# A fused three-layer kernel on one core: a new order of the first three weight strips, x in smaller pieces, ten idle matmuls, and the first norm's sum on another engine

## The chip, the cores and the metric

The kernel runs on one core of one Trainium2 chip. A core has a tensor engine (PE, matrix products, results in the PSUM banks), a vector engine (DVE), a scalar engine (ACT), GpSimd (POOL) and a sync engine (SP) that mostly issues DMAs. Each engine runs its own instructions in order, and they meet by semaphores. The metric is the device time of one execution in microseconds; lower is better. The kernel before took 1658.15 us, the median of three runs (1657.92 to 1658.49).

## The reference

Three transformer layers on x of 512 tokens by 1024 features, all in float32. What the change touches is the first step of layer 0:

```python
mem_n = rmsnorm(mem, mem_norm)
mem_kv = mem_n @ w_mem_kv[i]                      # keys and values of the memory attention
h = rmsnorm(x, norm_mix[i])
proj = h @ a_w_in[i]
u, b_gate, c_gate, q_mem = jnp.split(proj, [768, 1536, 2304], axis=-1)
y_tok = _short_conv(u, b_gate, c_gate, a_conv_w[i])   # b_gate * conv3(c_gate * u)
y_mem = _mem_attention(q_mem, mk, mv)
x = x + jnp.concatenate([y_tok, y_mem], axis=-1) @ w_out
```

A gated FFN, a layer with sliding-window attention, a second FFN, and a layer with sparse attention and retention follow. The change leaves them alone.

## The kernel before

**Arithmetic.** Activations lie feature-major: x is eight tiles (k = 0..7) of 128 features by 512 tokens. A product in float32 is made of three faster ones. An operand is split into a rounded high half and the rest: for the weight `w_hi` (a copy on ACT) and `w_lo = raw - w_hi` (DVE), for the activation `a_hi` (ACT, x times the norm's gain) and `a_lo` (DVE). A **strip** n is 128 output features: one weight block of 512 KB, and for each k three matmuls, hi·hi, hi·lo and lo·hi, 24 in all, into one PSUM bank. The rms factor of a token is multiplied in afterwards, when DVE reads the bank (`l0_epilogue`), so PE may start before the norm is known.

**The norm.** ACT squares the tiles of x into two buffers `sq`, POOL adds them up in `acc` (`squares`), PE sums `acc` over the features (`sums`, four matmuls of one column), DVE scales (`variance`), POOL raises to the power -1/2 (`power`), DVE makes a diagonal (`diagonal`, `diag`), PE spreads it over the partitions (`spread`), and ACT copies it to `rstd`.

**Strips.** Strips 0 and 1 are the memory queries, 2 to 4 the first conv triple (u, c, b), 5 to 12 keys and values of the memory (256 columns each), 13 to 27 the other conv triples. Strip n uses slot n % 2 of `w_hi` and `w_lo` and slot n % 4 of `raw`. ACT's `split(n)` waits until strip n - 2 has left PE (`blk_done`), DVE's follows ACT's, and SP's `load(n)` waits until DVE has split strip n - 3.

**The order.** Each engine has its list written out in the source. At the outset SP and ACT issue the transfers of x (four pieces of 512 KB, two tiles each) and of the first weights; PE runs strip 0, then strip 1, and so on; the sums of the first norm stand before strip 3 and its spread before strip 4. On ACT, `conv_out(0)` (the high half `y_hi` of the first conv tile) stands at n = 5 of its loop, and the squares of the memory in pairs at n = 4 to 7.

Of the kernel before, what the change touches and what calls it, by code (L numbers as in the profile page):

```python
# [102 lines left out]
def build(nc, a, out):  # L103
# [393 lines left out]
    with nc.Block() as block:  # L497
# [88 lines left out]
        def _(pool):  # L586
# [95 lines left out]
        def _(act):  # L682
            act.dma_start(gains[:], a["gains"]).then_inc(gains_in, 16)
            for j in (0, 2):
                act.dma_start(x[:, 2 * j:2 * j + 2, :], a["xT"][:, 2 * j:2 * j + 2, :])\
                    .then_inc(x_in[j], 16)
# [98 lines left out]
            for n in range(N_QM0, N_OUT0 + 1):  # L785
# [1691 lines left out]
```

## Time and profile before

| what | value |
|---|---|
| median of three runs | 1658.15 us |
| the profiled execution: its own time | 1657.95 us |
| its span in the trace | 1656.0 us |
| PE busy | 1621.1 us (98%) |
| DVE, ACT, POOL busy | 872.4, 572.6, 139.4 us |
| granted clock of PE, mean | 0.997 |
| DMA, mean over the span | 92 GB/s |

The span is what the trace covers; the execution's own time is 1.95 us longer. PE is matrix products, PEld the loading of weights beside them; a name with q, as SPq, is the engine's sequencer issuing DMAs. A row of the timeline begins with start and duration in us; in brackets stands how long the engine was idle before, and what ended that. A matmul's duration contains its drain, so successive ones overlap; their pitch is read from the starts.

### The profile page before, as it was taken

What the parts mean: (1) busy time and instruction counts of PE and PEld (TensorE: products, weight loads), DVE (VectorE), ACT (ScalarE), POOL (GpSimd) and SP (SyncE); (2) the same over time, 40 slices, a digit from 0 to 9 for tenths busy, and PEclk for the clock granted to TensorE, in tenths of its full rate; (3) what the DMA queues carried; (4) which work ended last, traced back from release to release, by engine and by line L of the source; (5) the groups of instructions that cost most, each with busy time, mean ns of one, the idle gap of its engine ahead of it and who ended that gap; (6) DMA issues with size and microseconds to landing.
All of it is one profiled execution on the core that took longest, in us unless ns stands there. A gap on an engine that the chain in (4) does not pass through costs nothing.

```text
span 1656.0 us, 20546 instructions
## 1 busy us (share of the span) xinstructions
PE 1621.1 (98%) x7706; PEld 1299.1 (78%) x7706; DVE 872.4 (53%) x1174; ACT 572.6 (35%) x965; POOL 139.4 (8%) x123
## 2 busy tenths in 40 slices
PE   7999999999999999999999999999999999999997
PEld 6877888888888876678888888887677677888885
DVE  5566654444523466764444443337666655555443
ACT  5333432232222345543323323322355541233222
POOL 3100200000000000030000001113211101000001
PEclk9999999999999999999999999999999999999999
DMA  5322323222333331132322332252111111233231
GB/s 213 128 76 89 97 90 101 99 91 101 113 105 99 69 111 33 38 110 89 101 100 90 101 123 95 88 203 66 64 54 50 51 64 32 83 103 100 90 102 77
DMA packets 43246, 152.70 MB, mean 92 GB/s; under 512 B 5325, under 2 KB 8622, under 8 KB 42670
## 3 DMA queue, kind: packets, MB, share of 16 engines
q1 hardware_dynamic: 42114, 148.36, 27.1%
q10 hardware_dynamic: 1068, 3.47, 0.7%
q8 instruction: 42, 0.69, 0.2%
q14 instruction: 22, 0.18, 0.0%
HBM read 149.42 MB, written 2.39 MB: 92 GB/s over the span
## 4 chain that ended last, share of the span: by engine, by line
PE 58%; DVE 3%; issue 1%; ACT 0%; POOL 0%; DVEq 0%; ACTq 0%; POOLq 0%
PE ps L1767 16%; PE ps L1769 15%; PE ps L1768 15%; PE ps L2114 1%; PE ps L2128 1%; PE ps L2150 1%; PE ps L2174 1%; PE ps L2214 1%; PE ps L2213 1%; PE ps L2215 1%; PE ps L1942 1%; PE ps L2062 0%; PE ps L1974 0%; PE ps L2164 0%; PE ps L1959 0%
## 5 line engine op out<-in xcount | busy, mean ns | idle before, releaser
L1767 PE MATMUL ps<-a_hi,w_hi 128*128 128x512 f32 (+1 forms) x1368 | 544.7, 398 | 10.9 <-DVE a_lo L1077 8.6
L1769 PE MATMUL ps<-a_hi,w_lo 128*128 128x512 f32 (+1 forms) x1368 | 534.6, 391 | 0.0
L1768 PE MATMUL ps<-a_lo,w_hi 128*128 128x512 f32 (+1 forms) x1368 | 534.5, 391 | 0.0
L1072 DVE TENSOR_TENSOR w_lo<-raw,w_hi 128x1024 fp32r<-128x1024 f32 (+4 forms) x262 | 334.6, 1277 | 257.7 <-ACT w_hi L695 252.2
L695 ACT ACTIVATE w_hi<-raw 128x1024 fp32r<-128x1024 f32 (+4 forms) x262 | 274.7, 1048 | 313.7 <-PE ps L1769 289.0
L1767 PEld LDWEIGHTS ps<-a_hi,w_hi 128*128 128x128 f32 (+1 forms) x1368 | 257.0, 188 | 73.3 <-issue 17.0
L1769 PEld LDWEIGHTS ps<-a_hi,w_lo 128*128 128x128 f32 (+1 forms) x1368 | 256.9, 188 | 55.3
L1768 PEld LDWEIGHTS ps<-a_lo,w_hi 128*128 128x128 f32 (+1 forms) x1368 | 257.2, 188 | 52.4 <-issue 1.0
L1098 DVE TENSOR_TENSOR tmp<-ps,rstd 128x512 f32<-128x512 f32 x121 | 83.4, 691 | 182.6 <-PE ps L1769 172.4
L1767 PE MATMUL ps<-g_hi,w_hi 128*128 128x512 f32 x352 | 137.0, 389 | 0.0
L1768 PE MATMUL ps<-g_lo,w_hi 128*128 128x512 f32 x352 | 137.0, 389 | 0.0
L1769 PE MATMUL ps<-g_hi,w_lo 128*128 128x512 f32 x352 | 137.0, 389 | 0.0
L602 POOL TENSOR_TENSOR acc<-acc,sq 128x512 f32<-128x512 f32 (+1 forms) x40 | 52.2, 1306 | 537.8 <-ACT sq L704 535.9
L845 ACT ACTIVATE g_hi<-tmp 128x512 f32 (+1 forms) x44 | 27.8, 632 | 198.6 <-DVE tmp L1272 198.6
L1767 PEld LDWEIGHTS ps<-g_hi,w_hi 128*128 128x128 f32 x352 | 66.1, 188 | 13.8
L1769 PEld LDWEIGHTS ps<-g_hi,w_lo 128*128 128x128 f32 x352 | 66.1, 188 | 13.8
L1768 PEld LDWEIGHTS ps<-g_lo,w_hi 128*128 128x128 f32 x352 | 66.1, 188 | 13.6
L1111 DVE TENSOR_TENSOR x<-x,ps 128x512 f32<-128x512 f32 (+1 forms) x40 | 27.4, 686 | 87.8 <-PE ps L1769 87.8
L841 ACT ACTIVATE tmp<-tmp 128x512 f32<-128x512 f32 x44 | 27.8, 632 | 122.8 <-DVE tmp L1098 122.8
L1077 DVE SCALAR_TENSOR_TENSOR a_lo<-x,gains,a_hi 128x512 fp32r<-128x512 f32 (+1 forms) x40 | 38.5, 973 | 33.8 <-ACT a_hi L707 33.8
L1276 DVE TENSOR_TENSOR g_lo<-tmp,g_hi 128x512 f32 (+1 forms) x44 | 30.5, 692 | 38.8 <-ACT g_hi L845 38.8
L707 ACT ACTIVATE a_hi<-x,gains 128x512 fp32r<-128x512 f32 (+1 forms) x40 | 28.1, 714 | 59.0 <-DVE x L1111 55.6
(271 smaller groups left out, 1739.8 us busy)
## 6 DMA issues: line engine op xcount, KB each, us to landing
raw<-w SPq DMA_DIRECT2D x135, 512.0 KB, 3.4
raw<-w8b SPq DMA_DIRECT2D x70, 512.0 KB, 3.4
raw<-w_down SPq DMA_DIRECT2D x32, 704.0 KB, 4.0
w<-cmp_w SPq DMA_DIRECT2D x2, 2048.0 KB, 10.9
raw<-w_out_first SPq DMA_DIRECT2D x8, 320.0 KB, 2.9
raw<-w_nsa_o SPq DMA_DIRECT2D x8, 256.0 KB, 2.6
out<-o_t SPq DMA_DIRECT2D x4, 512.0 KB, 3.2
bias<-rel_scratch SPq DMA_DIRECT2D x8, 192.0 KB, 7.1
```

The lines of the kernel that those rows point to most:

```text
L602: pool.tensor_tensor(acc[:, 0:cols], acc[:, 0:cols], sq[:, k % 2, 0:cols], ALU.add).then_inc(acc_ready, 1)
L695: act.activation(w_hi[:, slot, 0:w], raw[:, raw_slot, 0:w], ACT.Copy)\
L707: act.activation(a_hi[:, k, :], x[:, k, :], ACT.Copy, scale=gains[:, g, bass.ds(k, 1)])\
L841: act.activation(tmp[:, 2 * j, :], tmp[:, 2 * j, :], ACT.Silu).then_inc(silu_ready, 1)
L845: act.activation(g_hi[:, m, :], tmp[:, 2 * j + 1, :], ACT.Copy).then_inc(g_hi_ready, 1)
L1072: dve.tensor_tensor(w_lo[:, slot, 0:w], raw[:, raw_slot, 0:w], w_hi[:, slot, 0:w].bitcast(F32), ALU.subtract).then_inc(w_lo_ready, 1)
L1077: dve.scalar_tensor_tensor(a_lo[:, k, :], x[:, k, :], gains[:, g, bass.ds(k, 1)], a_hi[:, k, :].bitcast(F32), ALU.mult, ALU.subtract)\
L1098: ins = dve.tensor_tensor(dst, ps[:, bank, :], rstd[:], ALU.mult)
L1276: dve.tensor_tensor(g_lo[:, m, :], tmp[:, 2 * j + 1, :], g_hi[:, m, :].bitcast(F32), ALU.subtract)\
L1767: pe.matmul(o, wh, a_h, start=start and at == 0, stop=False)
L1768: pe.matmul(o, wh, a_l, start=False, stop=False)
L1769: ins = pe.matmul(o, wl, a_h, start=False, stop=stop and at == kt - 1)
```

## The change

- **x** comes in eight pieces of 256 KB, tile 0 on ACT's queue, the other seven on SP's. SP's queue begins with the gains and the first halves of weights 0 and 1; the second halves stand behind tile 3.
- **Strips 0 and 1** run side by side (`first_strips`): for each k three matmuls of strip 0, then three of strip 1. ACT and DVE split both weights in halves between the tiles of x.
- **Strip 2** has `third_hi` and `third_lo` in place of slot 0, so its split needn't wait for strip 0.
- **PE** begins with ten products of 128 columns of the all-ones tile, whose result nobody reads.
- **The first norm**: DVE adds the squares (`first_square`), not POOL. `sums` stands behind k = 6 of strip 2, `spread` behind k = 3 of strip 3.
- **Later pieces**: `conv_out(0)` and its low half move to n = 8 and 9; the squares of the memory move to n = 3 and 4, four at a time; the epilogues of strips 0 to 2 move from n = 4 to n = 3.

```diff
+WARM = 10
@@ SP
-            sp.dma_start(raw[:, 0, 0:mid], a["w8"][0][:, 0:mid]).then_inc(first_in, 16)
-            for j in (1, 3):
-                sp.dma_start(x[:, 2 * j:2 * j + 2, :], a["xT"][:, 2 * j:2 * j + 2, :]).then_inc(x_in[j], 16)
...
+            sp.dma_start(gains[:], a["gains"]).then_inc(gains_in, 16)
+            for n in range(2):
+                sp.dma_start(raw[:, n, 0:mid], a["w8"][n][:, 0:mid]).then_inc(first_in[n], 16)
+            for k in range(1, KT):
+                sp.dma_start(x[:, k, :], a["xT"][:, k, :]).then_inc(x_in[k], 16)
+                if k == 3:
+                    for n in range(2):
+                        sp.dma_start(raw[:, n, mid:KT * P], a["w8"][n][:, mid:KT * P]).then_inc(raw_in[n], 16)
@@ POOL
-            squares(V_MIX0)
+            clear(V_MIX0)
@@ ACT
-            act.dma_start(gains[:], a["gains"]).then_inc(gains_in, 16)
-            for j in (0, 2):
-                act.dma_start(x[:, 2 * j:2 * j + 2, :], a["xT"][:, 2 * j:2 * j + 2, :])\
-                    .then_inc(x_in[j], 16)
+            act.dma_start(x[:, 0, :], a["xT"][:, 0, :]).then_inc(x_in[0], 16)
...
+            act.wait_ge(raw_in[2], 16)
+            act.activation(third_hi[:], raw[:, 2, 0:KT * P], ACT.Copy).then_inc(w_hi_ready, 1)
             for k in range(KT):
                 square(V_MIX0, k, k % 2, x[:, k, :], first=k < 2)
-                if k == 3:
-                    split(2, KT * P)
+                if k == 5:
+                    split(3, KT * P)
@@ DVE
+            def first_square(k):
+                dve.wait_ge(sq_ready, k + 1)
+                dve.wait_ge(acc_ready, 1 + k)
+                dve.tensor_tensor(acc[:], acc[:], sq[:, k % 2, :], ALU.add).then_inc(acc_ready, 1)
@@ PE
+            def first_strips():
+
+                for k in range(KT):
+                    pe.wait_ge(a_lo_ready, k + 1)
+                    for n in range(2):
+                        if k == 0:
+                            pe.wait_ge(first_lo, n + 1)
+                        if k == KT // 2:
+                            pe.wait_ge(w_lo_ready, n + 1)
...
+                        pe.matmul(o, wh, a_hi[:, k, :], start=k == 0, stop=False)
+                        pe.matmul(o, wh, a_lo[:, k, :], start=False, stop=False)
+                        ins = pe.matmul(o, wl, a_hi[:, k, :], start=False, stop=k == KT - 1)
+            def begin_beside(n, at):
+
+                if n == 2 and at == 6:
+                    sums(V_MIX0)
+                if n == 3 and at == 3:
+                    spread(V_MIX0)
...
-            pe.wait_ge(half_ready, 1)
-            for n in range(N_QM0, N_OUT0):
+            for i in range(WARM):
+                pe.matmul(ps[:, stat_bank, 0:P], ones[:], ones[:], start=True, stop=True)
+            first_strips()
+            for n in range(N_CONV0, N_OUT0):
```

On DVE at the outset, before the change (`x4` is four in a row, the bracket names the semaphores waited for):

```order
L1144 TENSOR_TENSOR w_lo<-raw,w_hi 128x512 [waits first_hi]
L1077 SCALAR_TENSOR_TENSOR a_lo<-x,gains,a_hi 128x512 [waits a_hi_ready] x2
L1150 TENSOR_TENSOR w_lo<-raw,w_hi 128x512 [waits w_hi_ready]
L1077 SCALAR_TENSOR_TENSOR a_lo<-x,gains,a_hi 128x512 [waits a_hi_ready] x4
L1072 TENSOR_TENSOR w_lo<-raw,w_hi 128x1024 [waits w_hi_ready]
L1077 SCALAR_TENSOR_TENSOR a_lo<-x,gains,a_hi 128x512 [waits a_hi_ready] x2
L1072 TENSOR_TENSOR w_lo<-raw,w_hi 128x1024 [waits w_hi_ready]
L1226 SCALAR_TENSOR_TENSOR mem_lo<-memx,gains,mem_hi 128x256 [waits mem_hi_ready] x4
```

And after it:

```order
L1091 SCALAR_TENSOR_TENSOR a_lo<-x,gains,a_hi 128x512 [waits a_hi_ready]
L1160 TENSOR_TENSOR w_lo<-raw,w_hi 128x512 [waits first_hi] x2
L1091 SCALAR_TENSOR_TENSOR a_lo<-x,gains,a_hi 128x512 [waits a_hi_ready] x3
L1165 TENSOR_TENSOR w_lo<-raw,w_hi 128x512 [waits w_hi_ready] x2
L1091 SCALAR_TENSOR_TENSOR a_lo<-x,gains,a_hi 128x512 [waits a_hi_ready] x4
L1188 TENSOR_TENSOR third_lo<-raw,third_hi 128x1024 [waits w_hi_ready]
L1171 TENSOR_TENSOR acc<-acc,sq 128x512 [waits acc_ready,sq_ready] x8
L1086 TENSOR_TENSOR w_lo<-raw,w_hi 128x1024 [waits w_hi_ready]
L1175 SCALAR_TENSOR_TENSOR mem_lo<-memx,gains,mem_hi 128x256 [waits mem_hi_ready] x4
L1097 TENSOR_SCALAR var<-ps 128x4 [waits norm_sum]
L1175 SCALAR_TENSOR_TENSOR mem_lo<-memx,gains,mem_hi 128x256 [waits mem_hi_ready]
L1103 TENSOR_TENSOR diag<-ident,rs 128x512 [waits norm_pow,const_in]
```

The split of strip 1 moved forward among the tiles, and the eight sums now stand between the splits of strips 2 and 3.

On ACT from strip 5's split on, before the change (`y_hi` is `conv_out(0)`, `sq<-memx` a square of the memory):

```order
L695 ACTIVATE w_hi<-raw 128x1024 [waits blk_done,raw_in1]
L802 ACTIVATE table<-ps 12x383 [waits table_mm]
L804 ACTIVATE sinks<-sinks 128x12 [waits small_in]
L712 ACTIVATE rstd<-ps 128x512 [waits norm_spread]
L704 ACTIVATE sq<-memx 128x256 [waits acc_ready] x2
L695 ACTIVATE w_hi<-raw 128x1024 [waits blk_done,raw_in2]
L783 ACTIVATE y_hi<-y_s 128x512 [waits conv_step]
L704 ACTIVATE sq<-memx 128x256 [waits acc_ready] x2
L695 ACTIVATE w_hi<-raw 128x1024 [waits blk_done,raw_in3]
```

And after it:

```order
L698 ACTIVATE w_hi<-raw 128x1024 [waits blk_done,raw_in1]
L816 ACTIVATE table<-ps 12x383 [waits table_mm]
L818 ACTIVATE sinks<-sinks 128x12 [waits small_in]
L707 ACTIVATE sq<-memx 128x256 [waits acc_ready] x4
L698 ACTIVATE w_hi<-raw 128x1024 [waits blk_done,raw_in2]
L698 ACTIVATE w_hi<-raw 128x1024 [waits blk_done,raw_in3]
L698 ACTIVATE w_hi<-raw 128x1024 [waits blk_done,raw_in0]
L698 ACTIVATE w_hi<-raw 128x1024 [waits blk_done,raw_in1]
L795 ACTIVATE y_hi<-y_s 128x512 [waits conv_step]
```

`y_hi` moved from behind the split of strip 6 to behind that of strip 9, and no square stands between the splits of strips 6 to 9 any more.

## Rows read from the trace of the kernel before

**Rows 1.** The page, part 1: busy us (share of the span) xinstructions.

```profile
PE 1621.1 (98%) x7706; PEld 1299.1 (78%) x7706; DVE 872.4 (53%) x1174; ACT 572.6 (35%) x965; POOL 139.4 (8%) x123
```

**Rows 2.** Waits of PE: line, releaser, us in total, times, longest.

```profile
PE ps L1767 <- DVE a_lo L1077: 8.6, 1, 8.6
PE ps L1767 <- DVE w_lo L1072: 3.9, 5, 2.1
```

**Rows 3.** Timeline of PE at the outset.

```profile
8.63 0.77 PE L1767 MATMUL ps<-a_hi,w_hi 128*128 128x512 f32 x1 [8.63 <-DVE a_lo L1077]
...
14.71 0.39 PE L1769 MATMUL ps<-a_hi,w_lo 128*128 128x512 f32 x1
```

**Rows 4.** Timeline of PE, starts of strips 2, 3, 5, 7; sums and spread.

```profile
22.46 0.39 PE L1767 MATMUL ps<-a_hi,w_hi 128*128 128x512 f32 x1
...
27.90 0.95 PE L1779 MATMUL ps<-ones,acc 128*128 128x1 f32 x8
...
29.48 0.51 PE L1767 MATMUL ps<-a_hi,w_hi 128*128 128x512 f32 x1 [0.63 <-DVE w_lo L1072]
...
42.38 0.28 PE L1767 MATMUL ps<-mem_hi,w_hi 128*128 128x256 f32 x1
...
50.37 0.36 PE L1767 MATMUL ps<-mem_hi,w_hi 128*128 128x256 f32 x1 [2.08 <-DVE w_lo L1072]
...
54.38 0.58 PE L1779 MATMUL ps<-ones,acc 128*128 128x1 f32 x4 [0.91 <-POOL acc L602]
...
57.78 0.59 PE L1786 MATMUL ps<-diag,ones 128*128 128x256 f32 x2
```

**Rows 5.** DMA issues about 1.1 us: size, us from issue to landing.

```profile
x<-xT SPq DMA_DIRECT2D x1, 512.0 KB, 5.4
raw<-w SPq DMA_DIRECT2D x1, 256.0 KB, 2.8
gains<-gains ACTq DMA_DIRECT2D x1, 32.0 KB, 3.0
```

**Rows 6.** Windows, 10 to 12 us: busy us by engine, clock, DMA share, GB/s.

```profile
10.00:12.00 2.00, 2.00 (x6) 1.57 (x5) 2.00 (x4) 2.00 (x4) 0.00 (x0) 1.00 1.03 422
```

**Rows 7.** The page, part 6: count, size, median us to landing.

```profile
raw<-w_nsa_o SPq DMA_DIRECT2D x8, 256.0 KB, 2.6
```

**Rows 8.** Timeline of ACT, at the outset and at the first conv_out.

```profile
3.58 0.63 ACT L757 ACTIVATE w_hi<-raw 128x512 fp32r<-128x512 f32 x1
...
6.97 1.33 ACT L707 ACTIVATE a_hi<-x,gains 128x512 fp32r<-128x512 f32 x2 [2.77 <-DMA x<-xT]
...
46.31 0.63 ACT L783 ACTIVATE y_hi<-y_s 128x512 fp32r<-128x512 f32 x1 [2.62 <-DVE y_s L1190]
```

**Rows 9.** Timeline of DVE: a_lo, two splits, mem_lo, the two diags.

```profile
9.88 2.74 DVE L1077 SCALAR_TENSOR_TENSOR a_lo<-x,gains,a_hi 128x512 fp32r<-128x512 f32 x4
...
19.44 2.31 DVE L1072 TENSOR_TENSOR w_lo<-raw,w_hi 128x1024 fp32r<-128x1024 f32 x1 [4.23 <-ACT w_hi L695]
...
28.21 1.22 DVE L1072 TENSOR_TENSOR w_lo<-raw,w_hi 128x1024 fp32r<-128x1024 f32 x1
29.34 1.66 DVE L1226 SCALAR_TENSOR_TENSOR mem_lo<-memx,gains,mem_hi 128x256 fp32r<-128x256 f32 x4
...
33.43 0.69 DVE L1089 TENSOR_TENSOR diag<-ident,rs 128x512 f32<-128x512 f32 x1 [1.22 <-POOL rs L609]
...
56.78 0.43 DVE L1089 TENSOR_TENSOR diag<-ident,rs 128x256 f32<-128x256 f32 x1 [0.83 <-POOL rs L609]
```

**Rows 10.** Timeline of POOL: the first norm's eight sums, the power.

```profile
14.52 12.69 POOL L602 TENSOR_TENSOR acc<-acc,sq 128x512 f32<-128x512 f32 x8 [13.03 <-ACT sq L704]
32.29 1.03 POOL L609 TENSOR_TENSOR rs<-var,half 128x4 f32<-128x4 f32 x1 [5.08 <-DVE var L1083]
```

**Rows 11.** Groups of PE by form: busy us, mean ns of one.

```profile
L2164 PE MATMUL ps<-qr,kr 128*128 128x512 f32 x8 | 4.1, 592 | 0.0
...
L2164 PE MATMUL ps<-qr,kr 128*128 128x128 f32 x8 | 1.5, 274 | 0.0
```

More of the change, by code:

```diff
@@ L253, in build @@
     raw_in = [sem(f"raw_in{i}") for i in range(RAW)]
-    x_in = [sem(f"x_in{i}") for i in range(4)]
+    x_in = [sem(f"x_in{i}") for i in range(KT)]
     mem_in = sem("mem_in")
@@ L257, in build @@
     const_in = sem("const_in")
-    first_in = sem("first_in")
+    first_in = [sem(f"first_in{i}") for i in range(2)]
     first_hi = sem("first_hi")
@@ L792, in _ @@
                     mem_evac(0, MEM_AT[0][n - MEM_LAG[0]], 1)
-                if kind == "b":
+                if kind == "b" and i:
                     conv_out(i)
+                if n == 8:
+                    conv_out(0)
                 if n in (1, 2):
@@ L1146, in _ @@
             for k in range(KT):
                 operand(k, G_MIX0, k + 1)
[L1148 to L1154 removed]
+                if k == 0:
+                    first_half(0)
+                    first_half(1)
@@ new lines, in _, with conv_low @@
+                if k == 3:
+                    second_half(0)
+                    second_half(1)
+            dve.wait_ge(w_hi_ready, 3)
+            dve.tensor_tensor(third_lo[:], raw[:, 2, 0:KT * P], third_hi[:].bitcast(F32), ALU.subtract)                .then_inc(w_lo_ready, 1)
+            for k in range(KT):
+                first_square(k)
+            split(3, KT * P)
+            def conv_low(i):
+                dve.wait_ge(yc_hi_ready, i + 1)
+                dve.tensor_tensor(y_lo[:, i, :], y_s[:], y_hi[:, i, :].bitcast(F32), ALU.subtract)\
+                    .then_inc(yc_lo_ready, 1)
@@ L1759, in strip @@
                         pe.wait_ge(late[0], late[1])
-                    if isinstance(n, int) and n == 0 and k == kt // 2:
-                        pe.wait_ge(w_lo_ready, 1)
                     if ready:
                         pe.wait_ge(ready[0], ready[1] + k + 1)
-                    wh = w_hi[:, slot, k * rows:(k + 1) * rows]
-                    wl = w_lo[:, slot, k * rows:(k + 1) * rows]
+                    wh, wl = (third_hi, third_lo) if third else (w_hi[:, slot], w_lo[:, slot])
+                    wh, wl = wh[:, k * rows:(k + 1) * rows], wl[:, k * rows:(k + 1) * rows]
                     a_h, a_l = tiles[k] if tiles else (hi[:, k0 + k, 0:cols], lo[:, k0 + k, 0:cols])
@@ L1880, in _ @@
                 else:
-                    strip(n, a_hi, a_lo, bank_of(n), ready=(a_lo_ready, 0) if n == 0 else None,
-                          aside=(lambda at, n=n: mem_beside(0, n, at)) if n > N_CONV else None)
+                    strip(n, a_hi, a_lo, bank_of(n), third=n == N_CONV0,
+                          aside=lambda at, n=n: begin_beside(n, at))
             def out_phase(n0, late):
```

101 lines of the change are left out of this document (54 added, 47 removed).

## The prediction

> **What bounds the kernel now.** First the page: the tensor engine (PE) is busy 1621.1 of 1656.0 us [rows 1]. Everything else hides behind it, so time can only be won where PE stands still or runs slowly. Second the waits of PE: the largest by far is 8.6 us at the outset, then 3.9 us in five waits for a weight's low half [rows 2]; one more, 0.9 us, is for POOL's sum [rows 4]. Fourth the later PE rows, with strips counted by 24 matmuls: strip 2 starts at 22.46 and ends at 27.90; strip 3 starts only at 29.48; strip 7 waits until 50.37; the second norm's sums wait until 54.38; the spread of its result is at 57.78 [rows 4]. From 58 us on PE has 22.7 us without work in 1598, which this change doesn't touch.
>
> **The outset, before and after.** Before, ACT is ready at 3.6 but x arrives in 512 KB pieces, the earliest 5.4 us after issue; a_hi starts at 6.97 and PE at 8.63 [rows 3, 5, 8]. Now the first piece of x is 256 KB and first on ACT's queue (0.74). The like of it is the first half weight of before, 256 KB, 2.8 us from issue at 0.75, and gains took 3.0 us from the same moment [rows 5]; so a_hi of tile 0 starts at about 3.8. An a_hi takes about 0.67 us in a row, a half w_hi 0.63, an a_lo 0.69 in a row (0.75 alone), a half w_lo 0.69 like the diag of its size [rows 8, 9]. Chain: a_hi 3.8 to 4.5; a_lo 4.5 to 5.2 while ACT makes w_hi of strip 0 (its half weight is second on SP's queue, 1.19 + 2.8 = 4.0); w_lo 5.2 to 5.9; first real matmul at 5.95. That is 2.7 us earlier than 8.63.
>
> **Two strips side by side.** Each tile of x now feeds six matmuls, 1.36 us at the fast pitch, and costs DVE 0.69 us for its a_lo. DVE has four half weights in between, so a_lo of tile k is done at 7.45 (k=1), 8.2, 8.9, 11.0 (k=4), 11.7, 12.4 and 13.1; PE wants them at 7.5, 8.9, 10.2, 11.6, 12.9, 14.3, 15.7. The transfers keep ahead: the core moved 422 GB/s at 10 to 12 us [rows 6], 0.62 us for 256 KB, so the last piece of x (2.6 MB in all with the halves) lands at about 11.5. PE is the bound from 7.5 on, and both strips end at 17.0 at the fast pitch, against 22.46 at the strip counted above [rows 4]: 5.4 us gained, 2.6 from the start, 2.8 from the fourteen matmuls at 0.43 instead of 0.227.
>
> **The idle matmuls.** Ten plain fp32 products of 128 columns. The trace has none at the low clock. At the high one a record of 128 columns lasts 274 ns in the mean and one of 512 columns 592 [rows 11], so 384 columns cost 318 ns, two cycles a column; two records a product give 0.21 us, and 0.43 at 1.2 GHz: ten end at 1.0 + 4.3 = 5.3, before 5.95, and cost nothing. The other end: if each of the twenty weight loads stood beside its product instead of under it (pitch of sums, 0.12 us a record at the high clock, 0.24 at the low), they would end at 10.1 and hold PE by 4.1 us. I take 5.3, the value nearest to the rows: PE keeps its pitch of 512 columns with a load for each. What they buy is open too: the low level lasted 6.1 us of unbroken work before (8.63 to 14.71), and here 4.3 us of work, a gap of 0.7 us and then real work stand in its place. Below is nothing gained (fourteen slow matmuls), above all 2.8 us. Gaps of 2.1 and 0.9 us later did not lower the pitch: 0.12 us for 256 columns before and after them [rows 4]. I take the full 2.8, since the engine will have worked from 1.0 on but for that gap.
> The Trainium skill ("TensorE: Matmul & The Clock Gate", Part 1) says that the slow level is the default, that sustained activity lifts it, and that the monitor runs free of the kernel's start, so the number of slow matmuls differs between executions; no row here shows a second execution, but three times within 0.57 us speak for little of that.
>
> **The third strip and the first norm.** Its weight has a place of its own: ACT makes third_hi when raw 2 lands (about 12.7, after x) to 13.8, DVE third_lo 13.8 to 15.0. PE wants it at 17.0; covered by 2 us. Then the eight sums run on DVE: a two-input operation of 128x512 took 0.69 [rows 9], some 0.73 with the wait on each other (an estimate), while POOL's eight took 12.69 us in a row, 1.6 each [rows 10]. POOL is quiet now, and DVE's operations that ran beside it (a w_lo of 2.31 us instead of 1.22) return to their length [rows 9]. acc 0 to 5 end at 19.4; ACT's split of strip 3 comes after square 5 (which waits for acc 3, 17.9), at 18.5 to 19.5; squares 6 and 7 follow, acc 7 ends at 21.6, w_lo of strip 3 at 22.8. PE reaches the sums at 17.0 + 21 x 0.227 = 21.8, spends some 0.45 on them (0.58 with the drain, rows 4), and strip 3 starts at 22.9. Before, sums ended at 28.34 and strip 3 waited 1.1 us until 29.48. Gained so far: 6.6 us. DVE is now only 0.1 us ahead; this is what is late next.
>
> **A wait that is added.** The spread stands in the middle of strip 3, at 22.9 + 12 x 0.24 = 25.8. DVE's diag: four mem_lo at 0.42 (22.8 to 24.5), var 0.15, POOL's power 1.03 [rows 9, 10], one mem_lo under it, diag 0.69: 26.4. PE waits 0.6 us. Behind it on PE stand strips 3 and 4; rstd is later only than the epilogues want, and those were not waited for. Gain 6.0.
>
> **Strips 4 to 9.** Between the starts of strip 3 and strip 5 nothing else changes (29.48 to 42.38, 12.9 us). Before, ACT stood in the first conv_out (y_hi at 46.31, idle 2.6 us), and w_hi of strip 7 came only behind it; strip 6 ended at 48.1, and strip 7 waited until 50.37 [rows 4, 8]. Now conv_out(0) comes at n = 8 and the mem squares at n = 3 and 4, in slack. Strip 5 starts at 36.4, w_lo 6 is due 38.8 against a need at 39.3, w_lo 7 41.7 against 42.2. That wait goes: 2.2 more. The sums' wait for POOL (1.1 us) goes too, since POOL has long finished, but diag of that norm is bound to ACT's w_hi 9: strip 7's end + 3.9 us (53.3 to 57.2, [rows 4, 9]), while PE arrives at + 3.4. So 0.6 remains of 1.1. Total 6.0 + 2.2 + 0.6 = 8.8; y_lo (0.69) now stands ahead of the memory epilogues and may push w_lo 11 by 0.2. **Sum: 8.6 us.** The profiled execution took 1657.95 for its span of 1656.0, so 1649.35; the median is 0.2 higher, and I say 1649.4. What a measurement of this kernel can tell is about 0.2%, 3.3 us.
>
> **Rivals.** (a) The clock is still low at the first real matmul, and 14 are slow. Strips 0 and 1 end at 19.6, w_lo 3 at 24.1, strip 3 starts at 25.5 (4.0 gained); the added wait is hidden; total 4.0 + 2.2 + 0.6 - 0.2 = 6.6: 1651.4. For it: 0.7 us of gap and 4.3 us of work against 6.1 before. (b) The first operands come as late as before (5.4 us after issue, 6.1; PE at 8.3), other pieces crowding them: 2.3 less in front, 1651.7; with the slow clock 1654. For it: x of before met just three other transfers, here too many pieces are under way; against: both leading pieces are 256 KB and the first in line. (c) The burst holds PE until 10.1, after which the pitch is fast: 4.1 less, 1653.5; for it only that no row shows such products at the low clock. (d) Slower than before: small pieces that don't overlap. A 256 KB transfer by itself takes 2.6 us [rows 7]; twelve in line put raw 2's landing at 0.75 + 3.0 + 11 x 2.6 + 3.4 = 35.8, strip 2 at 38.1, the eight sums and w_lo 3 behind it at 45.4 against 29.48: +15.9, less the 2.4 of later waits: 1671. It decides from about 1.5 us a piece; the rows say 0.62, and four transfers were in flight together at the outset.
> The Trainium skill's "DMA: Bandwidth & Descriptors" ("Measured") asks for transfers of 1 MiB and calls small ones overhead-bound; that rule, taken for pieces in a row, is rival (d), and the trace's 422 GB/s with 512 KB pieces disagrees. (e) The front gain is real but strip 3 or 7 waits for DVE or ACT as long as PE is early: below 3.3 us in all, 1656; against it the slack of 0.5 us at strips 6 and 7, thin as it is.
>
> **How the numbers follow.** Forecast 0.50 (its own range 1648.3 to 1650.6), (a) 0.20, (b) 0.12, (c) 0.07, (e) 0.07, (d) 0.04. Range for 8 in 10: 1647.8, if the added waits don't appear, to 1653.6, where (a), (b) and (c) lie. Faster by over 0.2% (below 1654.8): the first four, 0.89; within: 0.06; slower 0.05.
>
> **What would show it.** First real matmul at about 6.0, pitch 0.23 at once; DVE gapless until 13; the end of 48 matmuls at 17.0; POOL without adds before the memory norm; strip 3 at 22.9; a wait of about 0.6 for diag; no wait at strip 7. A pitch of 0.43 in the side-by-side strips shows (a); x landing after 5 us (b); burst rows past 6 us (c); DMA under 300 GB/s with DVE idle between tiles (d); a wait for w_lo of over 1 us at strips 3, 6 or 7 (e).

## The result, and the profile after

The changed kernel takes 1650.34 us, the median of 5 executions (1648.82 to 1650.89), against 1658.15 (1657.92 to 1658.49): ratio 0.995, 95% interval 0.994 to 0.9961. Forecast was 1649.4, with a range of 1647.8 to 1653.6. Here and below disturbed executions (far above the others) are left out of medians and ratios. The profiled execution took 1648.91 us for a span of 1647.1; before it was 1657.95 for 1656.0.

PE's timeline of the changed kernel at the outset and in the first strips (start, length, engine, line, operation, count, and in brackets the idle time ahead with its releaser) answers to [rows 3, 4]:

```profile
1.00 4.63 PE L1906 MATMUL ps<-ones 128*128 128x128 f32 x20 [1.00 <-POOL ones L593]
6.60 0.47 PE L1823 MATMUL ps<-a_hi,w_hi 128*128 128x512 f32 x1 [0.97 <-DVE w_lo L1160]
8.21 0.50 PE L1823 MATMUL ps<-a_hi,w_hi 128*128 128x512 f32 x1 [0.67 <-DVE w_lo L1160]
...
18.66 0.39 PE L1804 MATMUL ps<-a_hi,third_hi 128*128 128x512 f32 x1
23.42 0.94 PE L1833 MATMUL ps<-ones,acc 128*128 128x1 f32 x8
24.23 0.49 PE L1804 MATMUL ps<-a_hi,third_hi 128*128 128x512 f32 x1
25.02 0.40 PE L1804 MATMUL ps<-a_hi,w_hi 128*128 128x512 f32 x1
28.08 1.13 PE L1840 MATMUL ps<-diag,ones 128*128 128x512 f32 x2
38.23 0.28 PE L1804 MATMUL ps<-mem_hi,w_hi 128*128 128x256 f32 x1
43.98 0.28 PE L1804 MATMUL ps<-mem_hi,w_hi 128*128 128x256 f32 x1
46.87 0.50 PE L1833 MATMUL ps<-ones,acc 128*128 128x1 f32 x4
50.82 0.70 PE L1840 MATMUL ps<-diag,ones 128*128 128x256 f32 x2 [0.48 <-DVE diag L1103]
```

The idle burst ends at 5.63, real work starts at 6.60, strip 2 (on third_hi) at 18.66, strip 3 at 25.02, strip 7 at 43.98 with no idle time ahead of it. The table sets the starts beside those of before (counted in the same way, 24 matmuls a strip) and beside the forecast:

| start of | before | forecast | after | gain forecast | gain measured |
|---|---|---|---|---|---|
| first real matmul | 8.63 | 5.95 | 6.60 | 2.7 | 2.0 |
| strip 2 | 22.46 | 17.0 | 18.66 | 5.4 | 3.8 |
| strip 3 | 29.48 | 22.9 | 25.02 | 6.6 | 4.5 |
| strip 5 | 42.38 | 36.4 | 38.23 | 6.0 | 4.1 |
| strip 7 | 50.37 | 42.2 | 43.98 | 8.2 | 6.4 |
| strip 9 | 58.02 | 49.4 | 51.17 | 8.6 | 6.9 |
| end of the span | 1656.0 | 1647.4 | 1647.1 | 8.6 | 8.9 |

The front gained 1.8 us less than forecast, and the end is right all the same. So about 2 us were gained far behind the change. PE's timeline shows most of them near 1400 us. Before:

```profile
1394.61 0.47 PE L1767 MATMUL ps<-ya_hi,w_hi 128*128 128x512 f32 x1
...
1399.87 1.37 PE L2186 MATMUL ps<-ident,on 128*128 128x128 f32 x8 [2.27 <-DVE on L1561]
1401.03 5.90 PE L2174 MATMUL ps<-vr,att 128*128 128x256 f32 x20
...
1413.79 0.47 PE L1767 MATMUL ps<-ya_hi,w_hi 128*128 128x512 f32 x1
```

and after, the same instructions:

```profile
1387.88 0.47 PE L1804 MATMUL ps<-ya_hi,w_hi 128*128 128x512 f32 x1
...
1393.14 1.06 PE L2247 MATMUL ps<-ident,on 128*128 128x128 f32 x8 [2.27 <-DVE on L1603]
1394.04 4.48 PE L2235 MATMUL ps<-vr,att 128*128 128x256 f32 x20
...
1405.39 0.48 PE L1804 MATMUL ps<-ya_hi,w_hi 128*128 128x512 f32 x1
```

Up to the wait the offset is 6.73 us (1394.61 less 1387.88), behind it 8.40. Both executions wait 2.27 us for the third head's normalised rows (on); then the same 20 products take 5.90 us before and 4.48 after. The windows (busy time and instructions of PE, weight loads, DVE, ACT and POOL, then granted clock, DMA share, GB/s) give the reason. Before:

```profile
1401.00:1404.00 3.00, 3.00 (x10) 2.43 (x9) 0.00 (x0) 0.60 (x1) 0.00 (x0) 0.52 0.00 0
0.00:8.00 8.00, 0.00 (x0) 0.00 (x0) 0.96 (x2) 3.07 (x5) 0.95 (x7) 1.00 0.77 261
```

After:

```profile
1393.00:1397.00 4.00, 3.86 (x22) 3.55 (x23) 0.64 (x2) 0.60 (x1) 0.00 (x0) 1.00 0.00 0
0.00:8.00 8.00, 5.57 (x23) 4.82 (x23) 1.90 (x3) 3.91 (x6) 0.95 (x7) 1.00 0.74 218
```

Before, the clock behind the wait is at its lower level (0.52), after it stays at 1.00. The second row of each is for the transfers: the first 8 us moved 218 GB/s where they had moved 261.

The rest comes at the very end. PE's last matmul starts 8.12 us earlier (1635.80 against 1643.92), the span ends 8.9 earlier, and the difference is in the stores of the output, before and after:

```profile
out<-o_t SPq DMA_DIRECT2D x4, 512.0 KB, 3.2
out<-o_t SPq DMA_DIRECT2D x4, 512.0 KB, 2.7
```

They are issued 2.8 us behind that matmul in both. From its start to the end of the span pass 12.0 to 12.1 us in the four traces of the kernel before and its variants, and 11.3 to 11.4 in the ten of the changed kernel and its variants. So 0.7 us belong to the change, though no edit touches the stores; why they land sooner stays open. The 8.9 us of the spans are then 6.9 at strip 9, 1.7 near 1400 us and 0.8 at the end, less 0.4 lost in small steps between.

The issues of the changed kernel at the outset (transfers, KB each, us from issue to landing) answer to [rows 5]:

```profile
x<-xT ACTq DMA_DIRECT2D x1, 256.0 KB, 3.5
...
raw<-w SPq DMA_DIRECT2D x1, 256.0 KB, 3.7
```

The leading 256 KB pieces land 3.5 and 3.7 us after issue; the sum had 2.8.

### The profile page after: what moved, and what is told of

The parts are those of the page before. It is cut to its first block, busy times and chain, and to the rows that moved or that the text cites. A ratio compares the mean times of both kernels' runs of the same rounds, so it can differ in the third digit from the quotient of the medians.

```text
span 1647.1 us, 20591 instructions
## 1 busy us (share of the span) xinstructions
PE 1621.8 (98%) x7726; PEld 1299.0 (79%) x7726; DVE 876.1 (53%) x1183; ACT 573.4 (35%) x966; POOL 127.1 (8%) x115
## 4 chain that ended last, share of the span: by engine, by line
PE 58%; DVE 3%; issue 1%; ACT 0%; POOL 0%; DVEq 0%; ACTq 0%; POOLq 0%
PE ps L1804 16%; PE ps L1806 15%; PE ps L1805 15%; PE ps L2175 1%; PE ps L2189 1%; PE ps L2211 1%; PE ps L2235 1%; PE ps L2275 1%; PE ps L2274 1%; PE ps L2276 1%; PE ps L2003 1%; PE ps L2123 0%; PE ps L2035 0%; PE ps L2225 0%; DVE w_lo L1086 0%
## 5 line engine op out<-in xcount | busy, mean ns | idle before, releaser
L1804 PE MATMUL ps<-a_hi,w_hi 128*128 128x512 f32 (+1 forms) x1344 | 533.6, 397 | 1.7 <-DVE w_lo L1086 0.4
L1806 PE MATMUL ps<-a_hi,w_lo 128*128 128x512 f32 (+1 forms) x1344 | 523.9, 390 | 0.0
L1805 PE MATMUL ps<-a_lo,w_hi 128*128 128x512 f32 (+1 forms) x1344 | 523.6, 390 | 0.0
L1086 DVE TENSOR_TENSOR w_lo<-raw,w_hi 128x1024 fp32r<-128x1024 f32 (+4 forms) x260 | 330.7, 1272 | 251.4 <-ACT w_hi L698 246.0
L1804 PEld LDWEIGHTS ps<-a_hi,w_hi 128*128 128x128 f32 (+1 forms) x1344 | 251.7, 187 | 64.0 <-issue 9.3
L1806 PEld LDWEIGHTS ps<-a_hi,w_lo 128*128 128x128 f32 (+1 forms) x1344 | 251.5, 187 | 54.5
L1805 PEld LDWEIGHTS ps<-a_lo,w_hi 128*128 128x128 f32 (+1 forms) x1344 | 251.9, 187 | 51.0 <-issue 1.0
L608 POOL TENSOR_TENSOR acc<-acc,sq 128x512 f32<-128x512 f32 (+1 forms) x32 | 39.8, 1245 | 514.7 <-ACT sq L707 513.8
L1806 PEld LDWEIGHTS ps<-g_hi,w_lo 128*128 128x128 f32 x352 | 66.1, 188 | 13.8
```

Of the source, the lines that this page charges most:

```text
L608: pool.tensor_tensor(acc[:, 0:cols], acc[:, 0:cols], sq[:, k % 2, 0:cols], ALU.add).then_inc(acc_ready, 1)
L1086: dve.tensor_tensor(w_lo[:, slot, 0:w], raw[:, raw_slot, 0:w], w_hi[:, slot, 0:w].bitcast(F32), ALU.subtract).then_inc(w_lo_ready, 1)
L1804: pe.matmul(o, wh, a_h, start=start and at == 0, stop=False)
L1805: pe.matmul(o, wh, a_l, start=False, stop=False)
L1806: ins = pe.matmul(o, wl, a_h, start=False, stop=stop and at == kt - 1)
```

## The experiments

Times are medians; ratios (with their 95% intervals) are against the kernel before, run beside each (1657.45 beside e1 to e4, 1659.63 beside e5 to e8, 1658.7 beside e9 to e11, 1657.99 beside e12), and are not the quotients of these medians. The changed kernel itself was not run beside them. Since its times, like most, fall into two groups (1648.82 and 1648.91; 1650.34 to 1650.89), the median jumps with the number in each, and like groups are compared where they can be told apart. Between sets of runs the lowest group of the kernel before shifts by 0.4 (1656.02 beside e1, 1656.40 beside e12), so smaller differences say nothing. Starts of strips are read as above, each from one trace; the three traces with the outset of the change (the change, e3, e9) have strip 2 at 18.46 to 18.66 and strip 9 at 50.71 to 51.62.

**The idle matmuls, taken out of the kernel after and put alone into the kernel before.**

```diff
# e1, after
-WARM = 10
+WARM = 0
# e2, before, ahead of the strips
+            for i in range(WARM):        # WARM = 10
+                pe.matmul(ps[:, stat_bank, 0:P], ones[:], ones[:], start=True, stop=True)
```

> The changed kernel without its ten idle matmuls, nothing else. Theory: they only bring the clock up before the first real matmul; without them the first 14 or so of the side-by-side matmuls have a pitch of 0.43 us, strip 2 starts 2.0 to 2.8 us later than 18.66, and the time rises by about 2 us, to 1650.9 or, with the low-clock stretch near 1400 us that the kernel before showed, 1652.6. Rival: real work alone brings the clock up as fast, since it is held back by operands anyway; strip 2 starts by 19.2 and the time stays at 1648.9 or 1650.6.

> The kernel before with the ten idle matmuls at the outset, nothing else. They end at about 5.6 us, and the first real matmul is at 8.63, a gap of 3 us. Theory: the clock is already up at 8.63 as in the changed kernel at 6.60, strip 2 starts at 19.7 instead of 22.46; part of it is kept: strip 3 waits for its weight behind POOL's sums and starts at 29.3, so only 0 to 1 us is won in all (1657.2 to 1658). Rival: the gap of 3 us lets the clock fall again and the pitch is 0.43 for some matmuls, strip 2 at 22.4, time 1658.1.

e1: 1649.25, five executions (0.9951, 0.9938 to 0.9963). e2: 1658.05 (1.0003, 0.9995 to 1.0012). PE's timeline of e1:

```profile
6.53 0.76 PE L1823 MATMUL ps<-a_hi,w_hi 128*128 128x512 f32 x1 [6.53 <-DVE w_lo L1160]
...
11.36 0.44 PE L1825 MATMUL ps<-a_hi,w_lo 128*128 128x512 f32 x1
11.63 0.40 PE L1823 MATMUL ps<-a_hi,w_hi 128*128 128x512 f32 x1
```

and of e2:

```profile
1.00 4.63 PE L1844 MATMUL ps<-ones 128*128 128x128 f32 x20 [1.00 <-POOL ones L588]
8.90 0.76 PE L1768 MATMUL ps<-a_hi,w_hi 128*128 128x512 f32 x1 [3.26 <-DVE a_lo L1078]
...
14.10 0.40 PE L1768 MATMUL ps<-a_hi,w_hi 128*128 128x512 f32 x1
```

Without the burst the first eleven matmuls run at a pitch of 0.43, until 11.4; with it the pitch is fast at once, so the burst does what it was put in for. But strip 2 starts at 19.84 instead of 18.66, 1.2 us later and not 2.8. Eleven slow matmuls cost 2.2 us by themselves; PE waits for operands in that stretch (0.67 us in the change), and slow matmuls fill time in which it would have waited. At strip 9 0.8 us are left (51.96 against 51.17), no more than like traces differ by. In the times the groups of e1 (1648.99 to 1649.25; 1651.11 and 1651.16) lie 0.2 and 0.5 above those of the change, also hardly more than the shift between sets. In e2 the burst ends at 5.63, 3.26 us pass without work, and the first real matmul is slow (0.76), with the pitch fast only from 14.1: nothing of the effect is left. Whether the clock had risen and fell in the gap, or had not risen, the trace doesn't tell, since the granted clock reads 1.00 at 9 to 13 us beside a pitch of 0.43, as it does at the outset of the kernel before.

**The first two strips one after the other.**

```diff
-                for k in range(KT):
-                    pe.wait_ge(a_lo_ready, k + 1)
-                    for n in range(2):
+                for n in range(2):
+                    for k in range(KT):
+                        pe.wait_ge(a_lo_ready, k + 1)
```

> The changed kernel with strip 0 run whole and then strip 1, all operands in the same order as now. Theory: PE waits for each a_lo in strip 0 (it ends at about 15.2) and has strip 1 still to do: strip 2 starts at 20.7 instead of 18.66, of which 0.3 is given back at the spread's wait: +1.7 us, 1650.6 or 1652.5. Rival: the operands of both weights are so late (w_lo of strip 1 at 8.15) that interleaving hides little: strip 2 by 19.3, +0.5.

1652.07 (0.9957, 0.9941 to 0.9974), four executions from 1650.28 to 1653.42. Strip 2 starts at 20.61, 1.95 later, strip 9 1.6 later; the median is 1.7 above. PE's timeline and one window of it:

```profile
8.44 0.75 PE L1823 MATMUL ps<-a_hi,w_hi 128*128 128x512 f32 x1 [0.95 <-DVE a_lo L1091]
```

```profile
9.00:11.00 2.00, 2.00 (x6) 1.41 (x5) 2.00 (x4) 1.99 (x4) 0.00 (x0) 0.50 1.04 392
```

With three matmuls a tile PE stands 0.95 us for the second a_lo, and the clock, which the burst had lifted, is low again (0.50) at 9 to 11 us; slow, PE then waits for no further a_lo. The change has a wait of 0.67 us there and keeps its pitch. It may be that the two strips side by side also spare PE this loss; one trace doesn't show it.

**The first norm's sums back on POOL.**

```diff
-            clear(V_MIX0)
+            squares(V_MIX0)
...
-            for k in range(KT):
-                first_square(k)
```

> The changed kernel with the first norm's eight sums back on POOL. Theory: POOL needs 1.3 to 1.6 us each from 15.7 on, ends at 26 to 28.5, and PE, which reaches the sums at 23.4, waits 3 to 5 us there; strip 3 at 28 to 30 instead of 25.0; +3 to +5 us (1652 to 1654), 1.7 more if the clock falls in that gap. Rival: the wait is hidden by the weight of strip 3 anyway, which DVE could now split at 23: +1 at most.

1656.79, nine executions (0.9993, 0.9983 to 1.0003). Its two groups (1656.07 to 1656.79; 1658.64 to 1659.38) lie 7.6 and 8.5 us above those of the change: this one edit undone takes back all of the 7.8. PE's timeline and a window:

```profile
28.60 1.86 PE L1831 MATMUL ps<-ones,acc 128*128 128x1 f32 x8 [5.27 <-POOL acc L608]
```

```profile
29.00:35.00 6.00, 6.00 (x18) 5.03 (x19) 4.12 (x9) 1.06 (x1) 1.67 (x2) 0.50 0.01 2
```

POOL's adds end at 28.6, however early PE is; strip 3 starts at 31.75 (6.7 later), and behind the wait the clock is at 0.50 for six microseconds, which makes it 7.9 at strip 9 (59.04). The expectation had the wait and not the whole of the clock. In the kernel before POOL ended at 27.21 [rows 10], just before PE came to the sums at 27.90 [rows 4], and cost PE nothing there. So this edit is a condition of the gain and not its source: it keeps what the earlier outset wins. It was not tried by itself in the kernel before.

**The third strip's weight in the shared place.**

```diff
-            act.activation(third_hi[:], raw[:, 2, 0:KT * P], ACT.Copy)
+            act.wait_ge(blk_done, 1)
+            act.activation(w_hi[:, 0, 0:KT * P], raw[:, 2, 0:KT * P], ACT.Copy)
...
-            dve.tensor_tensor(third_lo[:], raw[:, 2, 0:KT * P], ...)
+            dve.tensor_tensor(w_lo[:, 0, 0:KT * P], raw[:, 2, 0:KT * P], ...)
```

> The changed kernel with the third strip's weight in slot 0 again, so that ACT copies it only when strip 0 has left PE (18.4). Theory: strip 2 at 20.8 instead of 18.66; the squares stand behind that copy, the sums end at about 27.3 instead of 23.1, and strip 3 starts at 28.6 instead of 25.0: +3.6 us, 1652.5 or 1654.4. Rival: only the first 2.1 us count, since DVE had been waiting anyway: +2, 1650.9.

1652.76 (0.9964, 0.9952 to 0.9977), 2.4 above the change by the medians. But these stand in different groups: four executions of e8 (1651.99 to 1652.99) lie 3.6 above the lower group of the change, the other two (1654.10, 1654.83) 3.8 above the upper. PE's timeline:

```profile
20.01 0.50 PE L1805 MATMUL ps<-a_hi,w_hi 128*128 128x512 f32 x1 [1.79 <-DVE w_lo L1189]
...
26.66 1.05 PE L1834 MATMUL ps<-ones,acc 128*128 128x1 f32 x8 [1.60 <-DVE acc L1172]
```

PE waits 1.8 us for the weight and then 1.6 for the sums, since DVE does them behind it; strip 3 starts 3.3 us later and strip 9 3.4, as expected within 0.3.

**The first conv_out back at its old place.**

```diff
-                if kind == "b" and i:
+                if kind == "b":
                     conv_out(i)
-                if n == 8:
-                    conv_out(0)
...
-                    if i:
-                        conv_low(i)
+                    conv_low(i)
```

> The changed kernel with conv_out(0) and its low half back at their old places (ACT n = 5, DVE in the epilogue of strip 4), nothing else. Theory (prediction's step on strip 7): ACT stands in conv_out until DVE's y_s at 42.1, so w_hi of strip 7 comes at 42.8 instead of 41.4 and its w_lo ends at 45.0; strip 7 starts at 45.1 instead of 43.98, and the time rises by 1.1 us (the old wait was 2.1 because squares and POOL stood there too): 1650.0 without and 1651.8 with the low-clock stretch near 1400 us. Rival: ACT has slack enough now that the conv comes earlier; strip 7 stays at 44.0 and the time at 1648.9 or 1650.8.

1650.91 (0.9951, 0.9934 to 0.9967). PE and ACT in its timeline:

```profile
44.75 0.36 PE L1800 MATMUL ps<-mem_hi,w_hi 128*128 128x256 f32 x1 [1.01 <-DVE w_lo L1084]
```

```profile
41.76 0.63 ACT L795 ACTIVATE y_hi<-y_s 128x512 fp32r<-128x512 f32 x1 [2.62 <-DVE y_s L1230]
42.30 1.04 ACT L698 ACTIVATE w_hi<-raw 128x1024 fp32r<-128x1024 f32 x1
```

The chain is the one the prediction read from [rows 4, 8]: ACT idle 2.62 us in conv_out, w_hi of strip 7 behind it, PE 1.01 us late at strip 7. Worth: 1.2 us by strips (strip 5 was 0.41 early, strip 9 0.83 late), 0.6 by the medians of four and five executions.

**Idle matmuls in the wait near 1400 us, first try.** For the third head, behind the waits for the output's halves and ahead of the one for the norm:

```diff
# e3 in the kernel after, e4 in the kernel before
+                if h == 2:
+                    for i in range(FILL):        # FILL = 10
+                        pe.matmul(ps[:, 6, 0:P], ones[:], ones[:], start=True, stop=True)
                 pe.wait_ge(rt_norm, TB * h + TB)
```

> The changed kernel with ten more idle matmuls where the tensor engine waits 2.3 us for the third head's normalised rows (near 1390 us). Theory: the two levels of the changed kernel's times (1648.9 and 1650.8) are the low-clock stretch of 3.4 us that the kernel before shows at 1400.7, behind that wait; with the wait filled the stretch never comes, all runs are 1648.8 to 1649.2 and their granted clock is 0.998. Rival: the two levels come from the outset (slow matmuls in some executions); the fill changes nothing, and the times still spread over 2 us.

> The kernel before with the same ten idle matmuls in that wait, nothing else. Theory: its low-clock stretch goes in every execution, 1.7 us less: 1656.4, clock 0.998. Rival: the stretch has another cause, or the fill costs what it saves: 1658.1.

e3: 1652.77 (0.9967, 0.9954 to 0.998). e4: 1660.14 (1.0018, 1.0009 to 1.0027). Both were slower than without it. e3's timeline of PE and a window:

```profile
1393.54 3.66 PE L2247 MATMUL ps<-ones 128*128 128x128 f32 x20 [2.23 <-DVE ob L1609]
1396.99 1.56 PE L2251 MATMUL ps<-ident,on 128*128 128x128 f32 x8
```

```profile
1394.00:1398.00 4.00, 4.00 (x24) 4.00 (x23) 0.07 (x1) 0.00 (x0) 0.00 (x0) 0.58 0.00 0
```

The fill itself stands behind a wait of 2.23 us, for ob, which comes as late as on. So it filled nothing, ran at the low clock, and cost 2.4 us (e4: 2.7) by the medians. These two runs say nothing of the theory; the fill was misplaced.

**The fill where it can start at once.** Eight products into a bank that is free as soon as the attention's rows are out, ahead of all waits of the third head:

```diff
# e9 in the kernel after, e12 in the kernel before
+                if h == 2:
+                    pe.wait_ge(rt_att, TB * RH)
+                    for i in range(FILL):        # FILL = 8
+                        pe.matmul(ps[:, 2, 0:P], ones[:], ones[:], start=True, stop=True)
```

> The changed kernel with eight idle matmuls put into the tensor engine's 2.3 us wait near 1390 us, this time in a bank that is free as soon as the wait begins (the earlier fill stood behind a second wait and began when the first had ended). Theory: the low-clock stretch of 3.4 us near 1394 us follows that wait; with it filled, the level at 1650.8 disappears and all executions are near 1648.9, clock 0.998. Rival: the stretch isn't due to that wait; two levels 1.8 us apart remain.

> The kernel before with the eight idle matmuls of e9 in its own wait near 1397 us, nothing else. Theory: its low-clock stretch at 1400.5 goes in every execution, so its times lose the level about 1.8 us up and lie at 1656.2 (or 1658, where the clock falls in one of its gaps before strips 3 and 7 instead); set against e9 (1648.7) the change by itself is worth 7.3 to 7.6 us at least. Rival: the kernel before keeps its levels, since its low stretches come from other gaps: median 1658 as now.

e9: 1648.71 (0.994, 0.9926 to 0.9953). e12: 1657.81 (0.9996, 0.9987 to 1.0005). PE's timeline of e9:

```profile
1390.13 2.02 PE L2245 MATMUL ps<-ones 128*128 128x128 f32 x16
1392.56 1.06 PE L2252 MATMUL ps<-ident,on 128*128 128x128 f32 x8 [0.40 <-issue]
```

The wait is filled but for 0.40 us, and the transposes behind it take 1.06, as in the profiled execution of the change and not 1.37 as before. More telling are the five times: 1648.35, 1648.38, 1648.71, 1649.04, 1649.06, one cluster, as in e11 below. The change, e1 and e10, which lack the fill, have two clusters each, with 8 of 15 executions in the upper; with it none of 10 is. The kernel before has three: beside e12 its 15 executions lie at 1656.4 to 1657.1 (5), 1657.8 to 1658.2 (5) and 1659.5 to 1659.8 (5); with the fill the 11 lie at 1656.4 to 1656.5 (2) and 1657.8 to 1658.2 (9), and none in the highest (thin by itself: beside e1 only 1 of 22 without the fill stood there). So before has two places with such a stretch, and e12's windows show the other, behind the 1.15 us wait before strip 3:

```profile
30.00:33.00 3.00, 3.00 (x8) 2.30 (x7) 2.27 (x5) 0.15 (x1) 0.66 (x1) 0.50 0.52 179
```

The profiled executions agree, each with its place among the times. Without a stretch at either place are those of the change (1648.91), e8 (1651.99), e9 and e11, all in their lowest or only group. One stretch, near 1395 us, is in those of e1 (1651.16) and e10 (1649.37), both in their upper group; one is in those of before (1657.95, near 1400) and of e12 (1657.87, at 30), both in the middle group; and e2 (1660.07, the highest of its eleven) has it at both places. Its window near 1400 us:

```profile
1403.00:1406.00 3.00, 3.00 (x10) 2.33 (x9) 0.00 (x0) 0.60 (x1) 0.00 (x0) 0.54 0.00 0
```

**The transfers at the outset, and a version of everything found.** In e10, x in pieces of one, one, two, two and two tiles, and the first half of strip 1's weight on ACT's queue:

```diff
-            for n in range(2):
-                sp.dma_start(raw[:, n, 0:mid], a["w8"][n][:, 0:mid]).then_inc(first_in[n], 16)
-            for k in range(1, KT):
-                sp.dma_start(x[:, k, :], a["xT"][:, k, :]).then_inc(x_in[k], 16)
+            sp.dma_start(raw[:, 0, 0:mid], a["w8"][0][:, 0:mid]).then_inc(first_in[0], 16)
+            for k, w in ((1, 1), (2, 2), (4, 2), (6, 2)):
+                sp.dma_start(x[:, k:k + w, :], a["xT"][:, k:k + w, :]).then_inc(x_in[k], 16)
```

e11 is e10 with e9's fill, twelve idle products at the outset instead of ten, and each norm's variance ahead of the work that DVE did before it:

```diff
+                if n == 8:
+                    variance(V_MEM, EPS_A, 2)
...
                 if n == 1:
+                    variance(V_MIX0, EPS_A)
```

> The changed kernel with x in five pieces (tiles 0 and 1 alone, then pairs of 512 KB) and the first half of weight 1 second on ACT's queue, not third on SP's. Theory: that half weight landed at 6.8 and held w_lo of strip 1 until 8.15, because later pieces shared the DMA engines with it; issued 0.5 us earlier it lands near 5.8, strip 1's first matmul is at 7.2 to 7.5 instead of 8.21, strip 2 starts at 17.7 instead of 18.66: 0.9 us less at the front, about 0.6 in the time (1648.2 or 1650.0). Rival: the 16 engines are the limit whatever the order; strip 2 stays at 18.5 to 18.8 and the time at 1648.9 or 1650.8.

> All that the runs point to, on top of the changed kernel: the transfers of e10, twelve idle matmuls instead of ten, both norms' variance moved ahead of what DVE does beside it (ahead of four mem_lo for the first norm, ahead of w_lo 9 for the second), and the fill of e9. Theory: 0.6 at the front, 0.3 and 0.5 at the two spreads, and no low-clock stretch near 1394: 1647.5 in nearly every execution. Rival: the gaps are worth nothing since the next wait takes their place: 1648.9.

e10: 1649.35 (0.9939, 0.9925 to 0.9952). PE's timeline and two of its issues:

```profile
6.92 0.47 PE L1823 MATMUL ps<-a_hi,w_hi 128*128 128x512 f32 x1 [1.29 <-DVE w_lo L1160]
...
7.69 0.39 PE L1823 MATMUL ps<-a_hi,w_hi 128*128 128x512 f32 x1
```

```profile
raw<-w ACTq DMA_DIRECT2D x1, 256.0 KB, 4.4
raw<-w SPq DMA_DIRECT2D x1, 256.0 KB, 4.2
```

Strip 1's first matmul comes 0.5 us earlier (7.69 against 8.21) but the first of all 0.3 later, since strip 0's weight now takes 4.2 us beside strip 1's: the transfers share what moves in these microseconds. Strip 2 starts 0.35 earlier (18.31), where like traces differ by 0.2, but in e11, with the same transfers, it starts at 18.70. In the times e10's lower group (1647.75 and 1647.91) is 0.9 below e9, which ran beside it and has no stretch either; the starts account for little of that (strip 9 at 50.51 against 50.71), and the rest is open. e11: 1647.45 (0.9932, 0.9918 to 0.9945), five times from 1647.27 to 1647.67, the fastest of all and 1.3 below e9. In the first 60 us the waits listed for PE are those for the ones tile, one for w_lo (1.1 us) and one for a_lo (0.5); the wait for diag is gone, and strip 9 starts at 50.08, 1.1 earlier than in the change.

## Why the prediction was right, and where its steps were not

The forecast missed the median by 0.9 us and the profiled execution by 0.5. The mechanism held where it was tested: the earlier outset, DVE's sums, the third place and strip 7 are each seen in the starts and in a run. Two steps were wrong in size and lost 1.8 us up to strip 9, and that the end agrees so well is luck: 0.7 to 0.8 us came from the stores of the output, and in the profiled pair 1.7 more from a stretch at the low clock that only the execution of before had. The median of before and that of the change each stand in a group that has one such stretch by the traces, so for them the luck is the 0.8 us alone.

**The outset, mis-sized.** The step "2.8 us from issue" took a half weight of before as the like of x's first piece. With eight pieces of x and four halves under way it was 3.5 and 3.7, and a_hi started at 4.35. ACT, and then DVE, in the timeline of the change:

```profile
4.35 0.72 ACT L710 ACTIVATE a_hi<-x,gains 128x512 fp32r<-128x512 f32 x1 [1.67 <-DMA x<-xT]
...
6.79 0.63 ACT L762 ACTIVATE w_hi<-raw 128x512 fp32r<-128x512 f32 x1 [1.21 <-DMA raw<-w]
```

```profile
7.46 0.69 DVE L1160 TENSOR_TENSOR w_lo<-raw,w_hi 128x512 fp32r<-128x512 f32 x1 [1.00 <-ACT w_hi L762]
...
21.67 1.49 DVE L1171 TENSOR_TENSOR acc<-acc,sq 128x512 f32<-128x512 f32 x2 [0.57 <-ACT sq L707]
23.08 1.22 DVE L1086 TENSOR_TENSOR w_lo<-raw,w_hi 128x1024 fp32r<-128x1024 f32 x1
```

The larger error is "the transfers keep ahead", argued from 422 GB/s at 10 to 12 us [rows 6]: strip 1's first half weight lands only at 6.8, so PE waits 0.67 us for it at 8.21, and DVE's chain of a_lo starts late. Of the 1.7 us lost up to strip 2, 0.65 is the late first matmul, by the first landings, and about 1.0 this. Rival (b) named the mechanism with 2.3 us for the first landing; a third of it came true. Rival (d) did not occur: raw 2 was there before strip 2 asked for it, since its transfer ran beside the others.

**The idle matmuls: the state right, the price wrong.** They ended at 5.63 (forecast 5.3), cost nothing, and the clock was high at the first real matmul, so rivals (a) and (c) did not occur. But "2.8 from the fourteen matmuls" adds a faster PE to a PE that then waits: e1 puts the worth of the burst at 1.2 us at strip 2, and at strip 9 and in the times at no more than the scatter. Clock and operands were two bounds on one stretch, and I added their gains. The kernel before shows the same: by the pitch 14 matmuls are slow in its own trace and 7 in e4's, whose outset is the same, and yet strip 2 starts 13.8 us behind the first matmul in both.

**Third strip and first norm: right.** The weight was ready at strip 2 (no wait there), POOL's place in the chain is gone, and e7 and e8 give the worth of both parts beside all the others: 7.6 us and 3.6 (they overlap, since e8's cost is partly DVE's sums behind the weight, and like the costs of e1, e5 and e6 they don't add up to the gain). The four single-column sums cost 0.81 (23.42 to 24.23), not 0.45. On that 0.45 rest also the prediction's "ended at 28.34" and its wait of 1.1 us before strip 3 of the kernel before, where the row has 0.63 of idle time behind a drain [rows 4]. DVE's last adds end at 23.2 as its rows show, 1.6 later than forecast, but still ahead of PE, and strip 3's w_lo is done at 24.3, before PE comes to it at 25.02; PE had lost as much.

**The added wait.** Forecast 0.6 for diag; the spread came at 28.08 after some 0.3 of idle time. The second, 0.5 as forecast (0.48); e11 takes it away.

**Strip 7: right.** No wait at 43.98; e5 brings it back. The term was counted as 2.2 and was 2.2 between the kernels (the gain goes from 4.15 to 6.39); `conv_out(0)` alone, with everything else changed, is worth 1.0 there.

**What was missing: the stretches at the low clock.** The prediction had a granted clock of 1.00 from the window of [rows 6] and took the 2.27 us wait near 1400 us, like the other gaps of PE, as time that is lost once. It can be lost nearly twice: behind it PE may run at half speed for a while, worth 1.67 us (the two offsets above). In some executions it does, in others not. The profiled execution of before had it, that of after did not, and the 1.7 us stands in the difference of the spans though the change touched nothing there. The Trainium skill ("TensorE: Matmul & The Clock Gate", Part 1) says that the monitor runs free of the kernel's start, so that the number of slow matmuls differs between executions; for the outset I gave that little weight, and the traces bear the page out: with the outset of before unchanged, 14 matmuls are slow in its own trace, 10 in e12's and 7 in e4's. 1400 us later the clusters of times 1.8 us apart fit it too. Compared group by group, lowest with lowest, the change gains 7.2 to 7.6 us (1656.0 to 1656.4 against 1648.8), and with the wait near 1400 us filled in both 7.7 (1656.4 in e12, 1648.7 in e9). That is about the 6.9 of strip 9 and the 0.7 to 0.8 behind the last matmul.

That one of the two places went is the change's own doing: the wait before strip 3 (0.63 us in the profile of before, 1.15 in e2, e4 and e12) is gone, and with it the stretch behind it, which the profiles of e2 and e12 have at 30 us and none of those of the changed kernel and its variants but e7's, behind a wait of its own. That fits three groups of times before and two after. How often each occurs is too thinly sampled for an expected value: near 1400 us, three of the five times of the change.

## What to carry to other kernels

Where an engine is made faster and its operands earlier in one stretch, work the stretch out once with both, and never add the two gains; for the operands take the landing times at the rate of those very microseconds, not of a later, fuller stretch. When a sum agrees with the end but not with the starts on the way, look for the place where the offset jumps. And where times fall into clusters, look at the granted clock and the pitch behind PE's longest waits: in these runs filling one with idle products paid only where they were issued when the wait began (e9), not behind a second wait (e3).

## What the hardware showed

- A wait of PE of 1.15 us (before strip 3: e2, e12) or 2.27 (near 1400 us: before, e1, e10) was followed by a stretch at the low clock, 0.50 to 0.58 in the windows, with 1.6 to 1.7 us lost. The same waits without it stand in e4 and in the change. Behind the 5.27 us of e7 stand six microseconds at 0.50.
- The burst of ten fp32 products at the outset takes 4.63 us in 20 records, 0.23 each, and in the fill at the high clock 16 records take 2.02. Behind the burst and a gap of 0.97 us the pitch was fast at once, behind one of 3.26 us (e2) it was 0.43 for twelve matmuls.
- The granted clock reads 1.00 over the first slow matmuls (pitch 0.43 in before, e1 and e2) and 0.50 over later ones (e6, e7, e12). At the outset only the pitch shows the low level.
- The Trainium skill ("TensorE: Matmul & The Clock Gate", "HAM oscillation") describes kernels whose waits for transfers let the clock fall again and again; the fall behind e7's wait of 5.27 us agrees. It speaks of longer gaps than those of 1.15 and 2.27 us, behind which the traces show the same here.
- With more and smaller pieces in flight less was moved at first, 218 GB/s against 261 in the first 8 us, and the leading piece took 3.5 us from issue where a half weight had taken 2.8. From 8 to 16 us the small pieces moved 410 GB/s.
- The four stores of the output, 512 KB each, took 3.2 or 3.3 us from issue to landing (median) in the four traces of the kernel before and its variants, and 2.7 in all ten of the changed kernel and its variants. Why is open.
